# Projection loop: sums per head as four 64x64 products, high parts of the split weights rounded by ScalarE

## What is computed

```python
h = concatenate([x, dx]) @ w_comb            # x and its difference to the token before
r, k, v, g, w_lo, a_lo = split(h)            # r, k, v, g: 2048 wide, 32 heads of 64
w = -softplus(-(w0 + tanh(w_lo) @ w2)) - 0.5
a = sigmoid(a0 + a_lo @ a2)
kk = k * k_k
kk = kk / maximum(norm(kk, axis=-1), 1e-12)  # a sum of squares per head
k = k * (1 + (a - 1) * k_a)
bonus = sum(r * k * r_k, axis=-1) * v        # a sum per head
```

## Time and profile before

| | |
|---|---|
| time before, median of 3 runs | 2551.66 us (2550.65 to 2557.18) |
| profiled execution, its own time | 2552.2 us |
| its span in the trace | 2549.9 us |
| mean granted TensorE clock | 0.925 |
| TensorE matmul busy | 2213.5 us (87%) |
| VectorE | 1401.9 us (55%) |
| GpSimd | 1207.3 us (47%) |
| ScalarE | 824.4 us (32%) |

### The profile page before, as it was taken

One profiled execution on the slowest core, in us unless ns is written; L12 is line 12 of the kernel. 1 busy time (PEld: TensorE's weight loads), 2 busy tenths in 40 slices (PEclk: granted clock), 3 DMA queues, 4 the chain that ended last, 5 costly groups with the idle time before them and its releaser, 6 DMA issues.

```text
span 2549.9 us, 56210 instructions
## 1 busy us (share of the span) xinstructions
PE 2213.5 (87%) x22038; PEld 1868.7 (73%) x22038; DVE 1401.9 (55%) x2028; ACT 824.4 (32%) x2139; POOL 1207.3 (47%) x708
## 2 busy tenths in 40 slices
PE   6799999988888989886867999999894999798876
PEld 4699989877777878775867976777694776565555
DVE  6766666666666566664445413445415172638655
ACT  1532233325545555453212222333201111211331
POOL 1366656633223132233855831222384897775134
PEclk8899999999988889896987999999897999899998
DMA  2233344372333233323211221000022221221001
GB/s 86 85 141 141 153 150 151 136 196 44 81 62 71 58 71 74 69 48 109 79 64 50 83 74 34 33 33 23 27 83 94 74 91 42 66 83 58 17 0 66
DMA packets 158904, 197.54 MB, mean 77 GB/s; under 512 B 120992, under 2 KB 123296, under 8 KB 156448
## 3 DMA queue, kind: packets, MB, share of 16 engines
q1 hardware_dynamic: 158752, 195.25, 25.2%
HBM read 156.24 MB, written 38.99 MB: 77 GB/s over the span
## 4 chain that ended last, share of the span: by engine, by line
PE 56%; DVE 11%; issue 5%; ACT 4%; POOL 1%; DVEq 1%; ACTq 0%; POOLq 0%
PE wide L797 9%; PE wide L1224 8%; PE wide L1225 8%; PE wide L1226 8%; PE wide L1701 4%; PE wide L1810 2%; PE wide L812 2%; PE wide L820 1%; PE wide L1586 1%; PE wide L1766 1%; DVE x_w L1022 1%; PE wide L814 1%; DVE b_and_k L1015 1%; PE wide L1794 1%; PE wide L2063 1%
## 5 line engine op out<-in xcount | busy, mean ns | idle before, releaser
L1077 POOL TENSOR_TENSOR n_levels<-n,masks 128x192 f32<-128x192 f32 (+1 forms) x96 | 117.8, 1239 | 437.5 <-ACT n L958 437.5
L1224 PE MATMUL wide<-mixed_high,w_high_rwkv_in 128*128 128x264 f32 x720 | 213.0, 296 | 27.8 <-ACT log_decay L435 18.9
L1226 PE MATMUL wide<-mixed_high,w_low_rwkv_in 128*128 128x264 f32 x720 | 207.5, 288 | 0.0
L1341 DVE TENSOR_TENSOR sq_sum<-sq_sum,squares 128x528 f32<-128x528 f32 (+1 forms) x54 | 87.3, 1617 | 178.6 <-ACT squares L1306 178.6
L1225 PE MATMUL wide<-u_low_second,w_high 128*128 128x512 f32 x464 | 185.5, 400 | 0.0
L1248 POOL TENSOR_TENSOR w_high<-weights,con 128x1024 fp32r<-128x1024 f32 x60 | 147.5, 2459 | 73.6 <-PE wide L1226 63.7
L355 PE MATMUL wide<-mixed_in,weights 128*128 128x264 f32 x672 | 158.7, 394 | 13.7 <-DVE mixed_in L325 12.3
L1224 PEld LDWEIGHTS wide<-mixed_high,w_high_rwkv_in 128*128 128x128 f32 x720 | 139.0, 193 | 36.2 <-ACT log_decay L435 25.1
L1251 POOL TENSOR_TENSOR w_low<-weights,w_high 128x1024 fp32r<-128x1024 f32 x60 | 157.6, 2627 | 4.7
L355 PEld LDWEIGHTS wide<-mixed_in,weights 128*128 128x128 f32 x672 | 128.9, 193 | 41.0 <-issue 9.5
L797 PE MATMUL wide<-x_w,n_levels 64*64 64x64 f32 x2752 | 121.8, 231 | 37.8 <-DVE x_w L1022 21.0
(11 more groups left out here) (325 smaller groups left out, 6495.0 us busy)
## 6 DMA issues: line engine op xcount, KB each, us to landing
weights<-in_stream SPq DMA_DIRECT2D x200, 512.0 KB, 3.3
forms<-form SPq DMA_DIRECT2D x16, 2020.5 KB, 6.3
forms_in<-forms SPq DMA_DIRECT2D x96, 144.0 KB, 4.5
forms_in<-forms SPq DMA_DIRECT2D x32, 288.0 KB, 4.5
gate_bonus<-forms SPq DMA_DIRECT2D x16, 576.0 KB, 4.0
r_ahat_r<-forms SPq DMA_DIRECT2D x32, 144.0 KB, 3.1
mixed<-gate_bonus SPq DMA_DIRECT2D x14, 264.0 KB, 2.1
gated<-mixed SPq DMA_DIRECT2D x14, 264.0 KB, 4.8
```

The costliest lines, as they stand in the source:

```text
L1077: return pool.tensor_tensor(n_lvl[:, first:last, grp(g), :], n_all[:, grp(g), :].unsqueeze(1).to_broadcast([P, n, GC, C]), b_con[:, 1 + fi ...
L1224: pe.matmul(dst, w[0], x[0], start=start, stop=False)
L1226: return pe.matmul(dst, w[1], x[0], start=False, stop=stop)
```

## The change

It does two things, both in the projection loop.

The sums per head (kk and rk) are no longer two products of 128x128 by 264 columns, but four of 64x64: each head has its own rows of input, and for the second bank the outputs change places (head 0's sums of the second half go to rows 64 to 127, head 1's to rows 0 to 63). So ScalarE's root and VectorE's bonus product are made in three pieces each: one of 128 rows for the first half and two of 64 rows for the second. A new semaphore `sums_first` is raised by head 0's two products and waited for by both readers; TensorE also raises `sums_turn` ahead of the four.

The high parts of the split weights are written by ScalarE (`act_weights`, a copy to fp32r) in place of GpSimd's product with one. For pairs 1 to 15 the k and r weights are done at the head of `act_pair`, the v weights after the copy of k. GpSimd keeps the subtraction and waits for `w_high` alone. In pair 1 the head of `act_pair` comes after `act_in_parts`.

```diff
--- before.py
+++ after.py
@@ -276,7 +276,7 @@
 
         a_sems = {n: sem("a_" + n) for n in (
             "diff", "lerp", "lora_loaded", "lora_low", "proj_w", "proj_a", "tanh_w", "tanh_a", "k_copied", "r_copied", "kk_squared",
-            "p_exp", "kk_summed", "kk_rooted", "v_copied", "g_tanh", "pc_copied", "rk_summed", "dve", "pool", "stored", "in_rounded", "in_rest", "in_whole")}
+            "p_exp", "kk_summed", "kk_rooted", "v_copied", "g_tanh", "pc_copied", "rk_summed", "dve", "pool", "stored", "in_rounded", "in_rest", "in_whole", "sums_first", "sums_turn")}
 
         def half_bias(n, pair):
             if isinstance(pair, int):
@@ -371,6 +371,24 @@
 
         LERP_OF = [("k", 2), ("r", 3), ("v", 0), ("g", 1)]
 
+        TWO = (slice(0, C), slice(C, P))
+
+        def head_sums(pe, dst, src):
+
+            pe.sem_inc(s["sums_turn"], 1)
+            for hd, rows in enumerate(TWO):
+                for b in range(2):
+                    mm = pe.matmul(dst[TWO[hd ^ b], b, 0:HALF], heads[rows, hd * C:(hd + 1) * C], src[rows, PAD + b * HALF:PAD + (b + 1) * HALF],
+                                   start=True, stop=True)
+                    if hd == 0:
+                        mm.then_inc(s["sums_first"], 1)
+            return mm
+
+        def summed_parts(src):
+
+            cols = [slice(PAD + b * HALF, PAD + (b + 1) * HALF) for b in range(2)]
+            return [(slice(0, P), cols[0], src[:, 0, 0:HALF])] + [(TWO[hd], cols[1], src[TWO[1 - hd], 1, 0:HALF]) for hd in range(2)]
+
         def pe_pair(pe, i, first):
             def project(j, dst, lerps):
                 if not first and j < SPLIT:
@@ -406,18 +424,24 @@
             project(2, wide[0], 5)
             pe.wait_ge(s["k_copied"], i + 1)
             pe.wait_ge(s["kk_squared"], i + 1)
-            for b in range(2):
-                mm = pe.matmul(wide[2][:, b, 0:HALF], heads, a_sq[:, PAD + b * HALF:PAD + (b + 1) * HALF], start=True, stop=True)
-            mm.then_inc(s["kk_summed"], 1)
+            head_sums(pe, wide[2], a_sq).then_inc(s["kk_summed"], 1)
             pe.wait_ge(s["tanh_a"], i + 1)
             project(3, wide[1], 6)
             pe.wait_ge(s["r_copied"], i + 1)
             pe.wait_ge(DVE_A.sem, DVE_A.at(i, 7))
-            for b in range(2):
-                mm = pe.matmul(wide[3][:, b, 0:HALF], heads, a_rk[:, PAD + b * HALF:PAD + (b + 1) * HALF], start=True, stop=True)
-            mm.then_inc(s["rk_summed"], 1)
+            head_sums(pe, wide[3], a_rk).then_inc(s["rk_summed"], 1)
+
+        def act_weights(act, i, j):
+
+            before, step = ((3, i - 1), (2, i - 1), (1, i))[j]
+            ring.wait_full(act, 1 + j, i)
+            ring.wait_used(act, before, step)
+            act.activation(w_in[0][:, (1 + j) % 2, :], ring.slot(1 + j), ACT.Copy).then_inc(w_high, 1)
 
         def act_pair(act, i, first):
+            if not first:
+                act_weights(act, i, 0)
+                act_weights(act, i, 1)
             if first:
                 act.wait_ge(const_set, N_SET)
                 act.wait_ge(applied, 1)
@@ -427,6 +451,8 @@
                 act.wait_ge(POOL_A.sem, POOL_A.before(i))
             ring.wait_used(act, 1, i)
             act.activation(real(a_k), wide[2][:, :, 0:HALF], ACT.Copy).then_inc(s["k_copied"], 1)
+            if not first:
+                act_weights(act, i, 2)
             act.wait_ge(DVE_A.sem, DVE_A.at(i, 1))
             act.activation(a_sq[:], a_kk[:], ACT.Square).then_inc(s["kk_squared"], 1)
             ring.wait_used(act, 2, i)
@@ -443,7 +469,10 @@
                 act.wait_ge(s["stored"], 16 * i)
             act.activation(real(f_v), wide[0][:, :, 0:HALF], ACT.Copy).then_inc(s["v_copied"], 1)
             act.wait_ge(s["kk_summed"], i + 1)
-            act.activation(real(a_inv), wide[2][:, :, 0:HALF], ACT.Sqrt).then_inc(s["kk_rooted"], 1)
+            act.wait_ge(s["sums_first"], 4 * i + 2)
+            for rows, cols, part in summed_parts(wide[2]):
+                ins = act.activation(a_inv[rows, cols], part, ACT.Sqrt)
+            ins.then_inc(s["kk_rooted"], 1)
             ring.wait_used(act, 4, i)
             act.activation(real(a_tg), wide[1][:, :, 0:HALF], ACT.Tanh, scale=0.5).then_inc(s["g_tanh"], 1)
             act.wait_ge(EXP_A.sem, EXP_A.at(i, 1))
@@ -515,7 +544,10 @@
 
             dve.wait_ge(s["v_copied"], i + 1)
             dve.wait_ge(s["rk_summed"], i + 1)
-            step(dve.tensor_tensor(real(f_bon), wide[3][:, :, 0:HALF], real(f_v), ALU.mult))
+            dve.wait_ge(s["sums_first"], 4 * i + 4)
+            for rows, cols, part in summed_parts(wide[3]):
+                ins = dve.tensor_tensor(f_bon[rows, cols], part, f_v[rows, cols], ALU.mult)
+            step(ins)
 
             dve.wait_ge(s["g_tanh"], i + 1)
             step(dve.scalar_tensor_tensor(real(f_sg), real(a_tg), 1.0, wide[1][:, :, 0:HALF], ALU.add, ALU.mult))
@@ -524,12 +556,8 @@
             if not first:
 
                 pool.wait_ge(s["lerp"], 6 * KD)
-                for j, (before, step) in enumerate(((3, i - 1), (2, i - 1), (1, i))):
+                for j in range(SPLIT):
                     load, at = 1 + j, (1 + j) % 2
-                    ring.wait_full(pool, load, i)
-                    ring.wait_used(pool, before, step)
-                    pool.tensor_tensor(w_in[0][:, at, :].rearrange("p (k n) -> p k n", k=KD), ring.slot(load).rearrange("p (k n) -> p k n", k=KD),
-                                       ones.unsqueeze(1).to_broadcast([P, KD, P]), ALU.mult).then_inc(w_high, 1)
                     pool.wait_ge(w_high, SPLIT * i + (j + 1 - SPLIT))
                     pool.tensor_tensor(w_in[1][:, at, :], ring.slot(load), w_in[0][:, at, :].bitcast(F32), ALU.subtract).then_inc(w_split, 1)
             pool.wait_ge(EXP_A.sem, EXP_A.at(i, 2))
```

## The result

The changed kernel takes 2643.83 us (median of 4 runs, 2638.96 to 2647.59), against 2552.24 us before: a ratio of 1.0354, 95% interval 1.033 to 1.0378. It is 92 us slower; the forecast was 2636, range 2604 to 2664. The profiled execution took 2639.0 us with a span of 2637.1 us, 87.2 us more than the span before.

A forecast was written before the change was run, and what follows sets the result against it. TensorE was taken to bound the projection loop, busy 27.7 of 28.6 us a pair. Boundaries with clock 14 x (3.8 + 1.8) = 78, pair 1 +9, sums -3: 2551.7 + 84 = 2636 us, range 2604 to 2664.

The forecast's parts named there:

- The chain at the boundary: Before pairs 2 to 15, k waits for g product, tanh, f_pc, ScalarE copy and GpSimd subtraction: 3.8 us each.
- The clock: TensorE's clock falls to half behind the pause before each k product: 1.8 us a boundary, at 14 boundaries.
- Pair 1: Its weight copies wait behind `act_in_parts`, so TensorE starts k at 115.9: cost 9 us (8 to 12).
- the relief: In pair 1, silent GpSimd lets VectorE and ScalarE speed up by some 4.5 us; `act_in_parts` ends near 112.3.
- The sums: Four overlapping 64x64 products take 0.65 to 0.75 us, gaining 0.2 us for the kk sums, 16 times: 3 us.
- The pieces: Root and bonus product in three pieces add some 0.5 us each, covered by ScalarE's idle time and VectorE's slack.
- Without it 0.5 us a pair would appear: Without the slack the pause adds at VectorE's pair end, the bonus product's pieces would cost 0.5 us a pair.
- Faster: Rival, chance 0.04: k copy runs in ScalarE's 4.1 us idle before the tanh of g, rounding costs nothing: about 2540.
- The sum: Whole kernel: 14 x (3.8 + 1.8) = 78, pair 1 +9, sums -3, together +84 us.

The follow-up runs named there:

- e2: Changed kernel with only the rounding on ScalarE; sums as two 128x128 products and readers whole, as before: 2629.59 us, ratio 1.0306.
- e4: Changed kernel plus nine unused 128x240 matmuls behind the rk sums, to keep TensorE working through most of the pause: 2617.51 us, ratio 1.0251.
- e1: Changed kernel with the rounding back on GpSimd; four-quadrant sums and readers in pieces stay: 2572.13 us, ratio 1.0077.
- e3: Changed kernel with the next pair's k and r weight copies before the tanh of g (pair 1's ahead of `act_in_parts`): 2548.84 us, ratio 0.9996; again 2554.69, 0.9997.
- e6: Changed kernel with only pair 1's k and r weight copies moved ahead of `act_in_parts`: 2636.4 us, ratio 1.032.
- e7: Changed kernel with the k weights' high part back on GpSimd, r and v still on ScalarE: 2591.64 us, ratio 1.0138.

## Why the prediction was right, and where its terms were off

**The chain at the boundary: right, one duration off.** Each link came as told. The copy of 1024 columns takes 1.05 us (estimate 1.05). From the end of the g product to the k product it takes 4.66 us, 0.54 before: 4.12 more, predicted 3.8. The difference is the first subtraction, 2.84 us for 2.52: the estimate took the median of a line that stood elsewhere, and here it runs beside VectorE's tail. e2, with a shorter tail, has 2.37. The prediction's bound (2.40 to 2.78) had not reached it.

**The clock: right.** It fell to half at all 14 boundaries, for 3.4 us each, and e4 took it away alone: 1.5 us a pair for an estimate of 1.8. e2 shows how near the edge this lies: after pauses of 3.31 us it fell 11 times of 14.

**Pair 1: right in size.** k starts 117.24 (forecast 115.9), the copy of v 9.9 us later than before (forecast 9). 0.9 us of both was an offset from the start of the kernel, and `act_in_parts` ended 0.6 us later than the relief promised.

**The sums: mis-sized.** The four quadrants overlap, eight records in 0.68 us, four of them starting within 0.02 us. But the gain is 0.09 us a sum, not 0.2: counted from the last matmul of v to the second of g it took 1.23 us before and 1.15 after. The way in takes 0.21 us (274.95 to 275.16), for 0.12 between records of the v product; the way out takes 0.31 from the last sum to the first of g and 0.33 from that to its second, for 0.22 each. Estimated from the steps of 0.22 us, two in place of four would save 0.44 us; with 0.09 left, the change of shape costs some 0.35 in all, where the prediction had 0.2 to 0.3 for both ways. Over 16 pairs, that is 1.4 us, not 3.

**The pieces: right here, wrong by its own measure elsewhere.** In the changed kernel they are covered, as told, but for 1.7 us in front of the scan. "Without it 0.5 us a pair would appear" failed: e1 lost 1.3 us a pair. The prediction let the root's pieces cost nothing, as ScalarE idles behind them; but VectorE's chain starts from the root and moves with it, into GpSimd's subtraction. It also named the k copy as what waits for VectorE's end, where the r product waits too and is on the path. The tail had 0.2 us to spare. That slack, read from the end of VectorE's last step and the start of the r product, would have told.

**The rival that nearly mattered.** "Faster" asked for the k copy in the idle time before the tanh, and priced it at about 2540. e3 did that, and is neither faster nor slower than before: the condition was the right one, the price too good, since the sums bring 0.09 and not 0.2 us, the pieces cost 1.6 us in front of the scan, and pair 1's copy of v starts only 0.1 to 0.4 us earlier than before, where up to 4.6 had been allowed for.

**The sum.** 14 x (4.06 + 1.47 - 0.09) = 76.2, pair 1 9.9, the scan's front 1.7, the rest -0.7: 87.2 by the spans (87.1 in these rounded terms), forecast 84. Some of this closeness is luck: over the 14 turns the chain was put 4.5 us too low (3.8 for 4.12) and the clock 4.6 too high (1.8 for 1.47). The medians differ by 92; the profiled execution is the fastest of the four runs. In what stands behind the scan the single runs differ, and that part was not looked into.

**Open:** why e6's gain is 8.7 us by the ratios and 12.3 by the spans (the interval of the ratio is 4 us wide to either side), what differs behind the scan, and which pause lets the clock fall. After 4.06 us it always fell, after 3.31 us mostly, and e7 had it once in 14 turns with pauses of 1.99 us.

## What to carry to other kernels

Free time of an engine counts only from where its own program stands. Before a step is moved to an idle engine, look at what is queued ahead of it there and what that waits for: the same three copies cost 92 us behind the tanh of g and nothing ahead of it. A wait that shows once in a loop turn on a busy TensorE may be paid twice, in the pause and in the clock behind it. Splitting a reader to speed up a product pays only after the reader's own slack has been measured: 0.09 us won on TensorE, 0.6 us paid on each reader.

## What the runs showed of the hardware

- VectorE and GpSimd slow each other: VectorE's step of 0.43 us took 2.65 (e1) and 2.57 us (e7) beside a GpSimd operation, one of 0.76 us 2.67; GpSimd's subtraction of 2.37 us took 2.84 to 2.88 beside VectorE's tail. Not every step is slowed: the reciprocal takes 3.45 us with GpSimd busy beside all of it (the kernel before) and with GpSimd idle (the changed one). A groups view averages such sizes away.
- Products of 64 by 64 on all four quadrants run at once, also where two of them write one bank. Going from whole products to them and back eats most of what they save: from the first record of a kk sum to the first of g it takes 0.61 us with four quadrants and 0.89 with whole products, but 0.09 us of the difference arrives.
- The clock fell in step with the loop, 0.09 to 0.38 us after TensorE had resumed and not during the pause, in each of 14 turns. The delay is not fixed: in e2 it was 0.18 to 1.51 us. The Trainium skill (TensorE: Matmul & The Clock Gate, "HAM oscillation — how this bites in real kernels") describes such a fall once a loop turn. The trace agrees, with 0.50 for 3.4 us and then 1.00.
